# Gate logits and branch products of a two-layer encoder with 128-token stationary tiles and 512 moving weight columns

## What is computed

```python
h = rms_norm(x, norm1_g[layer])
proj = h @ w_in[layer]            # q, k, v of three mixers, then 3 x 1024 gate logits gl
ya, yb, yc = ...                  # differential, banded and stick-breaking attention, each (B, S, 512)
branches = jnp.stack([ya, yb, yc], axis=2)
up = jnp.einsum('bsnw,nwd->bsnd', branches, w_branch[layer])
gates = jax.nn.sigmoid(gl.reshape(B, S, N_BRANCH, D))
merged = jnp.sum(gates * up, axis=2)
x = x + merged @ w_out[layer]
x = x + peer(rms_norm(x, norm2_g[layer]), ...)
```

## Time and profile before

| | |
|---|---|
| median of three runs | 2165.88 us (2164.99 to 2166.47) |
| the profiled execution, its time | 2167.15 us |
| its span, first to last instruction | 2165.3 us |
| PE busy | 2153.0 us, 99% |
| DVE busy | 1545.7 us, 71% |
| ACT busy | 1195.5 us, 55% |
| POOL busy | 706.6 us, 33% |
| DMA | 377.25 MB, mean 174 GB/s |

### The profile page before, as it was taken

The page is one execution under the profiler, slowest core; times in us unless marked ns, Lnnn a source line. Parts: engine busy times, 40 slices in busy tenths (PEclk is TensorE's granted clock), DMA queues, the critical chain, the costliest instruction groups (busy, mean ns, idle before and its releaser), DMA issues.

```text
span 2165.3 us, 40750 instructions
## 1 busy us (share of the span) xinstructions
PE 2153.0 (99%) x13860; PEld 1943.4 (90%) x13860; DVE 1545.7 (71%) x2760; ACT 1195.5 (55%) x1972; POOL 706.6 (33%) x342
## 2 busy tenths in 40 slices
PE   8999999999999999999999999999999999999999
PEld 6789989999999988888877899899999999888887
DVE  5767868977777766666567678699777786666665
ACT  5755555477777533333367544454777885333332
POOL 1400006887777500000023000178777774000000
PEclk9999999999999999999999999999999999999999
DMA  6444554555555555555654445545555555555554
GB/s 229 149 145 144 176 187 144 185 175 165 164 160 161 175 194 193 194 193 194 195 191 154 147 147 186 171 150 184 174 158 164 164 159 178 194 192 193 193 193 155
DMA packets 103763, 377.25 MB, mean 174 GB/s; under 512 B 11760, under 2 KB 11760, under 8 KB 103152
## 3 DMA queue, kind: packets, MB, share of 16 engines
q1 hardware_dynamic: 102528, 371.24, 53.8%
q10 hardware_dynamic: 1136, 4.79, 0.6%
HBM read 374.94 MB, written 1.05 MB: 174 GB/s over the span
## 4 chain that ended last, share of the span: by engine, by line
PE 98%; DVE 1%; ACT 0%; DMA 0%; issue 0%; SPq 0%; ACTq 0%; DVEq 0%
PE ps L501 29%; PE ps L502 29%; PE ps L503 29%; PE ps L838 3%; PE ps L509 3%; PE ps L520 1%; PE ps L511 1%; PE ps L644 1%; PE ps L799 1%; PE ps L617 0%; PE ps L605 0%; PE ps L716 0%; DMA raw<-in_stream 0%; PE ps L709 0%; DVE hT L1269 0%; PE ps L632 0%
## 5 line engine op out<-in xcount | busy, mean ns | idle before, releaser
L1121 ACT ACTIVATE w_hi<-raw 128x1024 fp32r<-128x1024 f32 x512 | 523.5, 1054 | 438.3 <-PE ps L503 437.9
L486 POOL TENSOR_TENSOR w_lo<-raw,w_hi 128x1024 fp32r<-128x1024 f32 x264 | 634.0, 2416 | 268.9 <-ACT w_hi L1121 268.9
L501 PE MATMUL ps<-hT,w_hi 128*128 128x256 f32 x2432 | 692.4, 285 | 0.0
L502 PE MATMUL ps<-hT,w_hi 128*128 128x256 f32 x2432 | 688.1, 283 | 0.0
L503 PE MATMUL ps<-hT,w_lo 128*128 128x256 f32 x2432 | 688.0, 283 | 0.0
L501 PEld LDWEIGHTS ps<-hT,w_hi 128*128 128x128 f32 x2432 | 466.7, 192 | 2.1 <-issue 2.1
L502 PEld LDWEIGHTS ps<-hT,w_hi 128*128 128x128 f32 x2432 | 466.7, 192 | 0.1
L503 PEld LDWEIGHTS ps<-hT,w_lo 128*128 128x128 f32 x2432 | 466.5, 192 | 0.0
L501 PE MATMUL ps<-w_hi,wgt_hi 128*128 128x512 f32 x1024 | 398.5, 389 | 0.0
L503 PE MATMUL ps<-w_hi,wgt_lo 128*128 128x512 f32 x1024 | 398.4, 389 | 0.0
L502 PE MATMUL ps<-w_lo,wgt_hi 128*128 128x512 f32 x1024 | 398.4, 389 | 0.0
(11 more groups left out here) (194 smaller groups left out, 2834.5 us busy)
## 6 DMA issues: line engine op xcount, KB each, us to landing
raw<-in_w_u SPq DMA_DIRECT2D x256, 512.0 KB, 3.5
raw<-in_w_v SPq DMA_DIRECT2D x256, 512.0 KB, 3.7
raw<-in_stream SPq DMA_DIRECT2D x192, 512.0 KB, 3.6
arena<-in_bias ACTq DMA_DIRECT2D x2, 1024.0 KB, 6.2
arena<-in_subk ACTq DMA_DIRECT2D x2, 1024.0 KB, 6.1
x<-in_x SPq DMA_DIRECT2D x4, 256.0 KB, 4.9
out<-x SPq DMA_DIRECT2D x4, 256.0 KB, 2.1
arena<-in_params ACTq DMA_DIRECT2D x2, 283.5 KB, 3.4
```

Source lines behind the costliest of these rows:

```text
L486: nc.gpsimd.tensor_tensor(w_lo[:, i, :], raw[:, i, :], w_hi[:, i, :].bitcast(F), ALU.subtract).then_inc(early_ready.sem, 1)
L501: mm(out_, left[0], right[0], start=start, stop=False, skip_group_check=group)
L502: mm(out_, left[0], right[1], start=False, stop=False, skip_group_check=group)
L1121: f(w_hi[:, slot, :], raw[:, slot, :], ACT.Copy).then_inc(hi_ready.sem, 1)
```

## The change

Gate logits and branch products are done by token: 128 tokens stationary, 512 weight columns moving, 12 matmuls per slot in place of 24. The host lays these weights out accordingly. What follows from it:

- The gates have tokens on partitions, so `rstd` is a column of factors. `spread(0)`, `make_diag(0)` and the copy of it go. A block of four slots fills bank 6 (tokens 0 to 127) and bank 7 (tokens 128 to 255); DVE takes bank 6 and ACT bank 7, 6 times each in a layer. The next block writes the same two banks.
- A branch result of 512 columns takes two slots, in the banks 0/1 and 2/3 in turn. DVE multiplies and adds after the odd slots, both token tiles.
- `merged` has tokens on partitions. PE turns it (`merged_transposes`, four tiles of 4 transposes): two behind branch slot 10, two inside slot 1 of the output projection. DVE splits the turned tiles out of PSUM (`split_merged`).

```diff
-                def by_feature(bank, n0, signal, parts=(0, 1)):
...
                 def gate_slot(n):
 
-                    g, c2 = n // 2, n % 2
-                    if g < 2:
+                    cb, k = n // 4, n % 4
+                    slot = N_QKV + n
+                    if n == 0:
                         pe.wait_ge(yc_ready.sem, yc_ready.at(layer, 2))
-                    elif c2 == 0:
-                        pe.wait_ge(gate_ev.sem, gate_ev.at(layer, g - 1))
-                    by_feature(6 + g % 2, N_QKV + 2 * g, gate_mm, (c2,))
+                    pe.wait_ge(w_ready.sem, w_ready.at(layer, slot + 1))
+                    for t in range(TT):
+                        if k == 0 and cb:
+                            pe.wait_ge(gate_ev[t].sem, gate_ev[t].at(layer, cb))
+                        for kc in range(2):
+                            last = product(ps[:, 6 + t, :],
+                                           [a[:, 2 * k + kc, t * P:(t + 1) * P] for a in (hT_hi, hT_lo)],
+                                           [w[:, slot % SLOTS, kc * 512:(kc + 1) * 512] for w in (w_hi, w_lo)],
+                                           start=(k == 0 and kc == 0), stop=(k == 3 and kc == 1))
...
+                def merged_transposes(n):
+
+                    t, half = n % 2, n // 2
+                    pe.wait_ge(merged_whole.sem, merged_whole.at(layer, n + 1))
+                    transposes(ps[:, (6, 7, 0, 1)[n], :], merged[:, t, half * 512:(half + 1) * 512], 4
+                               ).then_inc(mergedT_mm.sem, 1)
+
                 for u in range(12):
...
+                    for t in range(TT):
+                        if u == 0:
+                            pe.wait_ge(yb_ready.sem, yb_ready.at(layer, t + 1))
+                        if k == 0 and g >= 2:
+                            pe.wait_ge(up_taken.sem, up_taken.at(layer, 2 * g + t - 3))
+                        for w2 in range(2):
+                            last = product(ps[:, 2 * (g % 2) + t, :],
+                                           [y_parts[UP_ORDER[u // 4]][:, part, 2 * k + w2, t * P:(t + 1) * P] for part in range(2)],
+                                           [w[:, n % SLOTS, w2 * 512:(w2 + 1) * 512] for w in (w_hi, w_lo)],
+                                           start=(k == 0 and w2 == 0), stop=(k == 1 and w2 == 1))
...
+                    if u == 10:
+                        merged_transposes(0)
+                        merged_transposes(1)
+
                 def merged_wait(k, t):
 
-                    if t == 0:
-                        pe.wait_ge(merged_ready.sem, merged_ready.at(layer, k + 1))
+                    if k == 1:
+                        merged_transposes(2 + t)
+                    if k % 2 == 0:
+                        pe.wait_ge(merged_ready.sem, merged_ready.at(layer, k + t + 1))
...
+                def take_gate(cb):
+
+                    if cb is not None:
+                        act.wait_ge(gate_mm.sem, gate_mm.at(layer, 2 * cb + 2))
+                        f(gate_tile(cb, 1), ps[:, 7, :], ACT.Copy, scale=rstd[:, 1:2]).then_inc(gate_ev[1].sem, 1)
...
-                def take_gate(g):
-
-                    dve.wait_ge(spread_ready.sem, spread_ready.at(layer, 1))
-                    dve.wait_ge(gate_mm.sem, gate_mm.at(layer, g + 1))
-                    v.tensor_tensor(gates[:, 2 * g:2 * g + 2, :], ps[:, 6 + g % 2, :].rearrange("p (a b) -> p a b", a=2),
-                                    rstd_b[:].unsqueeze(1).broadcast_to([P, 2, T]), ALU.mult).then_inc(gate_ev.sem, 1)
+                def take_gate(cb):
+
+                    if cb is not None:
+                        dve.wait_ge(gate_mm.sem, gate_mm.at(layer, 2 * cb + 1))
+                        v.tensor_scalar(gate_tile(cb, 0), ps[:, 6, :], rstd[:, 0:1], None, ALU.mult
+                                        ).then_inc(gate_ev[0].sem, 1)
...
+                def take_up(u, t):
+
+                    b, half = UP_ORDER[u // 4], (u // 2) % 2
+                    at = slice(half * 512, (half + 1) * 512)
+                    o = 2 * (u // 2) + t
+                    dve.wait_ge(up_mm.sem, up_mm.at(layer, o + 1))
+                    part = merged[:, t, at]
+                    dst = part if u < 4 else upt[:, t, :]
+                    v.tensor_tensor(dst, ps[:, 2 * ((u // 2) % 2) + t, :], gates[:, b, t, at], ALU.mult
+                                    ).then_inc(up_taken.sem, 1)
+                    if u >= 4:
+
+                        dve.wait_ge(up_taken.sem, up_taken.at(layer, o + 1))
+                        dve.wait_ge(dve_chain, own.n)
+                        last = v.tensor_tensor(part, part, dst, ALU.add)
...
+                def split_merged(n):
+
+                    t, half = n % 2, n // 2
+                    dve.wait_ge(mergedT_mm.sem, mergedT_mm.at(layer, n + 1))
+                    tile = ps[:, (6, 7, 0, 1)[n], :].rearrange("p (a b) -> p a b", a=4)
...
                 for u in range(12):
                     split((N_STREAM - N_WQ - N_OUT - N_BR + u + SLOTS,))
...
+                    if u % 2:
+                        for t in range(TT):
+                            take_up(u, t)
+                    if u == 10:
+                        split_merged(0)
+                        split_merged(1)
...
+                    if n == 0:
+                        split_merged(2)
+                        split_merged(3)
```

More of the change, by code:

```diff
@@ L175, in build @@
         qkT = view(QKT, 6, 4, T)
-        gates = view(GATE, 24, T)
+        gates = view(GATE, 3, TT, D)
         yT = view(YT, 3, 4, T)
-        merged = view(MRG, KC, T)
+        merged = view(MRG, TT, D)
         bias = view(BIAS, B_HEADS, T)
@@ L256, in build @@
         gate_mm = Signal(sem("gate_mm"), 12)
-        gate_ev = Signal(sem("gate_ev"), 12)
+        gate_ev = [Signal(sem(f"gate_ev{t}"), 6) for t in range(TT)]
         sq_ready = Signal(sem("sq_ready"), 8)
@@ L352, in fill_key, with block_end, gate_tile @@
             return KEYS - N_EARLY - 2 * (pair + 1)
+        def block_end(i, second):
+            n = STEP_FROM[i] + second
+            return n // 4 if n < STEP_FROM[i + 1] and n % 4 == 3 else None
+        def gate_tile(cb, t):
+            return gates[:, cb // 2, t, (cb % 2) * 512:(cb % 2 + 1) * 512]
         def c_heads(c):
@@ L534, in _, with spread @@
             for layer in range(LAYERS):
-                def spread(which):
+                def spread():
                     pe.wait_ge(masks_ready.sem, masks_ready.at(layer, 1))
-                    pe.wait_ge(diag_ready.sem, diag_ready.at(layer, which + 1))
-                    mm(ps[:, (7, 0)[which], 0:T], ones, diag[:].rearrange("p t q -> p (t q)"), start=True, stop=True
+                    pe.wait_ge(diag_ready.sem, diag_ready.at(layer, 1))
+                    mm(ps[:, 0, 0:T], ones, diag[:].rearrange("p t q -> p (t q)"), start=True, stop=True
                        ).then_inc(spread_mm.sem, 1)
@@ L955, in round_tiles, with take_spread @@
                         round_h(n)
-                def take_spread(which):
-                    act.wait_ge(spread_mm.sem, spread_mm.at(layer, which + 1))
-                    f(rstd_b[:], ps[:, (7, 0)[which], 0:T], ACT.Copy).then_inc(spread_ready.sem, 1)
+                def take_spread():
+                    act.wait_ge(spread_mm.sem, spread_mm.at(layer, 1))
+                    f(rstd_b[:], ps[:, 0, 0:T], ACT.Copy).then_inc(spread_ready.sem, 1)
                 split(0)
@@ L1106, in _ @@
                 take_yb(1)
[L1107 removed]
+                for t in range(TT):
+                    act.wait_ge(gate_ev[t].sem, gate_ev[t].at(layer, 6))
                 for b in UP_ORDER:
[L1109 to L1110 removed]
+                    whole = gates[:, b, :, :].rearrange("p t d -> p (t d)")
+                    f(whole, whole, ACT.Sigmoid).then_inc(gate_ready.sem, 1)
                 for n in range(N_STREAM - N_WQ - N_OUT - N_BR, N_STREAM - N_WQ):
@@ L1498, in _ @@
                 split_outputs(1, yb_ready)
+                def take_up(u, t):
[11 more added lines that the diff above has]
+                        last = v.tensor_tensor(part, part, dst, ALU.add)
+                        if u < 8:
+                            own.one(last.then_inc(dve_chain, 1))
+                        else:
+                            last.then_inc(merged_whole.sem, 1)
@@ new lines, in split_merged @@
+                def split_merged(n):
+                    t, half = n % 2, n // 2
+                    dve.wait_ge(mergedT_mm.sem, mergedT_mm.at(layer, n + 1))
+                    tile = ps[:, (6, 7, 0, 1)[n], :].rearrange("p (a b) -> p a b", a=4)
+                    hi, lo = (m[:, 4 * half:4 * half + 4, t * P:(t + 1) * P] for m in (m_hi, m_lo))
+                    own.one(v.tensor_copy(hi, tile).then_inc(dve_chain, 1))
+                    dve.wait_ge(dve_chain, own.n)
+                    v.tensor_tensor(lo, tile, hi.bitcast(F), ALU.subtract).then_inc(merged_ready.sem, 1)
@@ L1510, in _ @@
```

(15 more changed lines are left out.)

75 lines of the change are left out of this document (32 added, 43 removed).

## The result

The changed kernel takes 2172.61 us (median of 9 runs, 2171.22 to 2173.44) against 2166.25 us before (9 runs beside them, 2164.99 to 2166.72). The ratio is 1.003, with a 95% interval of 1.0021 to 1.0039: slower by some 6.4 us, 0.3%. The forecast was 2166.4 us; the result lies 0.6 us above the top of its range.

A forecast was written before the change was run, and what follows sets the result against it. PE's own stream was taken as the bound, busy 99% of the span. Per layer 5.0 us saved against 5.3 added gave +0.3, rounded to +0.5 in both layers: 2166.4 us on the median, range 2159.5 to 2172.0.

The forecast's parts named there:

- gate slots: Gate stage: 12 wide matmuls replace 24 narrow ones, saving 0.10 us in 14 slots and 0.14 in 10; 2.8 us a layer.
- branch slots: Branch products: 144 wide matmuls at 0.227 us and one entry take 32.8 us against 34.63; 1.8 us a layer saved.
- spread: Before the first wide products behind eight transposes: the spread goes, saving 0.44 us a layer.
- transposes: Branch stage and output projection: sixteen more transposes of merged rows with their entries add 1.9 us a layer.
- waits for merged rows: After branch slots 10 and 11's sums: PE waits 1.1, 0.9 and 1.1 us for DVE; 3.3 us a layer with hand-overs.
- ACT at the last step: Last attention step: ACT's new bank 7 copy stands ahead of the last probabilities' copy, delaying PE 0.1 us a layer.
- gates out of PSUM: Gate bank copies by DVE and ACT at five block turns: both have idle time, so no cost to PE.
- I cost this at nothing: Gate bank turns: bank 6 free 0.4 us before slot end, bank 7 0.9 after, wanted 1.36 into the next; zero cost.
- Rival C: Turn of the gate banks: copies 0.6 us late at five turns cost 3 us a layer, 2172.4 us; chance 0.12.
- The clock: Whole span: PE taken to run at the full granted clock, 2.4 GHz, in all 40 slices; no fall priced.
- Rival B: Gates and branches: wide matmuls run at 0.233 us, costing 5.2 us in both layers, 2171.6 us; chance 0.10.

The follow-up runs named there:

- gates first: Changed kernel with DVE and ACT copying gate banks before their weight splits, and ACT the last probabilities before the gates; 2168.76 us, 1.0012 of the kernel before.
- last kernel: Changed kernel with gate copies, all sums of merged rows and the merged rows' split out of PSUM ahead of weight splits; 2159.45 us, 0.997 of the kernel before.
- slot 9 only: Changed kernel with DVE forming the sums of branch slot 9 alone before its weight split; 2167.96 us, 1.0008 of the kernel before.

## Why the prediction was wrong

By its own terms, per layer, with what they measured:

| term | predicted | measured | from |
|---|---|---|---|
| gate slots | -2.8 | -2.6 | 88.45 - 86.04 without waits, and 2.96 - 2.81 in the first slot |
| branch slots | -1.8 | -1.8 | trains of 11.02, 10.88, 8.17 and 2.73 us (2.83 less the entry behind the transposes) against 34.63 |
| spread | -0.44 | -0.4 | layer 1's q, k, v stage |
| transposes | +1.9 | +1.8 | 0.89 in the branches; 24.12 - 23.25 in the projection without waits |
| waits for merged rows | +3.3 | +3.4 | (9.41 - 8.17) + (1.74 - 0.79) + (3.99 - 2.79) |
| ACT at the last step | +0.1 | +0.14 | 1.49 - 1.35 |
| gates out of PSUM | 0 | **+2.05** | the three turns above |
| clock fall | not in it | **+1.6**, layer 1 | 4.40 - 2.83 |

The six terms that were priced all hold within 0.3 us, the waits of the merged rows, which had the widest bounds, within 0.1. The terms add up to 2.6 us a layer, the landmarks of layer 0 give 2.7; with these the sum is 2 x 2.7 + 1.6 = 7.0 us. The changed kernel's profiled execution reached its gate stage 1.6 us earlier (133.07 against 134.67), 1.2 more than the spread accounts for, all of it in the first 30 us. That leaves 5.8 of the 6.0 by which the spans differ. The first products, behind the load of `x`, start 0.4 us earlier (10.12 against 10.48). The rest is the clock: they start at 0.43 us apart in both kernels, and go over to 0.23 within these twelve in the changed kernel, only behind them in the kernel before. The first eight transposes of `arena` start at 28.2 to 29.2 us in the eight profiled executions with the change and at 30.1 in the single one without it; one such execution can't tell whether this belongs to the change.

**The step that failed is "I cost this at nothing".** The argument was that DVE has bank 6 free 0.4 us before the slot ends and ACT bank 7 0.9 us behind it, since ACT's split starts 0.2 us behind PE's slot end. That figure came from the earlier trace rows, a branch slot, where ACT's queue holds nothing but splits. In the attention steps the split stands behind two exponents, and these behind DVE's maximum of the scores. So DVE's split, which waits for ACT's, starts 3.4 us behind the end of the slot that it refills (145.65 against 142.27) and not 1.3 as in the earlier trace rows, and the copy behind it is late as well. The data for the copy had been ready for that whole time; its place in the queue made it late. Rival C names this mechanism and gives 2172.4 us against 2172.61 measured; yet its price was 0.6 us at five turns, and the truth is 1.07, 0.52 and 0.46 at three. A third of its agreement is luck: 4.1 of its 6.0 us are there, and the 1.6 of the clock fill most of the rest. The kernel with gates first, whose turns cost nothing and whose clock still fell, took 2168.76 us, inside the range. Less the 1.6 us of the clock alone, the measured time would be 2171.0 us, inside as well; the turns are the larger of the two. It had 0.12 because the slack was counted, but counted with a row from another stage; a row of ACT in an attention step would have shown the exponents ahead of the split.

**The clock** was taken as given from a row of full slices. A wait of 1.1 us was priced at 1.1 us; two in a row, 0.4 us of transposes apart, cost 1.6 us more through the matmuls behind them.

**Rival B** (slow pace, 0.10) is settled for the branches by 0.227, and the output projection kept 0.233 behind the fast train. In the gate stage the distance is neither. Behind an entry it lies between 0.22 and 0.24 us for two to ten matmuls and then goes over to 0.227. In 21 of the 24 slots of layer 0 (without 1 and 2, which run together, and 8, which has a wait inside) the ten inner distances average 0.230. Slots ahead of scores take 2.93 us on average (2.81 to 2.97), as taken from the q, k, v stage (2.94); the others take 2.89 (2.84 to 2.95) where 2.82 had been taken, and that goes with the 0.2 us that the gate term lacks. What sets the two paces was not tried and stays open.

**What was right** is the value of the change without its waits: 2.6 + 1.8 + 0.4 - 1.8 = 3.0 us a layer, 6.0 in both. The last kernel measures 6.7 by the medians, and 6.4 in the profiled executions from the first eight transposes of `arena` to the end (30.11 to 2165.3 against 28.84 to 2157.6). It was lost in the queues: 2 x 3.4 us for merged rows, 2 x 2.05 for gates, 0.3 for the last step, 1.6 for the clock.

## What to carry to other kernels

When a change makes an engine wait for something new, take the latency of the producer from its queue at that very place: write down what stands ahead of it there, and what each of those waits for in turn. A split or copy for later use that waits on another engine belongs behind the operation whose input is ready and whose consumer is PE: in this kernel a few moves of that kind turned a change worth +0.3% into one worth -0.3%. After each move look for the next link: the wait for the sums (5.6 us in all) gave way to one for the split of the sums (2.2).

And where a kernel runs at full clock with PE never idle, a pair of stalls of a microsecond can cost more than its length, as it did in 24 of 31 runs here. Look at windows of a few us behind it, in every layer and in more than one run.

## What the runs showed of the hardware

- The granted clock fell from 2.4 to 1.2 GHz for some 3.4 us behind two waits (1.09 and 0.67 us), after 31 us of branch trains without a gap. From the end of the train of 36 to the next product PE did nothing for 3.0 us but eight transposes; with slot 9 only it was 1.3 us, and the clock stayed. Matmuls of 512 columns went from 0.227 to 0.43 us. The fall is not certain: the same program has it in no layer, one or both from run to run. The third wait alone (0.8 us in the kernel with slot 9 only) did not bring it about in any of ten runs.
- The wide matmul has two steady paces at full clock: 0.227 us in the branches (y_a, y_b, y_c stationary) and 0.233 in the output projection. The projection keeps 0.233 where its first slot follows the fast train with no wait between (last kernel: 12 in 2.79 us), and where it starts behind transposes (last kernel: 54 in 12.67). How the train is entered, which the prediction had supposed, does not decide it.
